# A two-layer decoder step with FFN in token halves: weight low parts and last pooling steps on VectorE, inverse root by logarithm on ScalarE, residual additions of x on GpSimd

## The reference, cut to what matters

```python
for i in range(2):
    h = rms_norm(x, norm_mix_pre[i]) * (1 + scale) + shift
    o = mla(h) if i == 0 else pool_mix(h)      # window sums of 2/4/8/16 rows, then a 256x256 product
    x = x + gate * rms_norm(o, norm_mix_post[i])
    h = rms_norm(x, norm_ffn_pre[i]) * (1 + scale_f) + shift_f
    u = h @ w_up                               # 1024 x 5632
    conv = b + u[t-2]*w0 + u[t-1]*w1 + u[t]*w2
    y = (silu(conv[:, :2816]) * conv[:, 2816:]) @ w_down
    x = x + gate_f * rms_norm(y, norm_ffn_post[i])
# pool_mix of group g with window w: (window_sum / min(pos + 1, w) - h) @ w_grp[g] * ls
```

## Time and profile before

| | |
|---|---|
| median of the runs | 2921.64 us |
| the profiled execution, its time | 2929.04 us |
| its span, first to last instruction | 2927.3 us |
| mean granted TensorE clock | 0.962 |
| TensorE matmul busy | 2586.9 us (88%) |
| VectorE busy | 1962.7 us (67%) |
| ScalarE busy | 1332.8 us (46%) |
| GpSimd busy | 518.9 us (18%) |

### The profile page before, as it was taken

The page is one execution under the profiler, slowest core; times in us unless marked ns, Lnnn a source line. Parts: engine busy times, 40 slices in busy tenths (PEclk is TensorE's granted clock), DMA queues, the critical chain, the costliest instruction groups (busy, mean ns, idle before and its releaser), DMA issues.

```text
span 2927.3 us, 49336 instructions
## 1 busy us (share of the span) xinstructions
PE 2586.9 (88%) x18538; PEld 2324.5 (79%) x18538; DVE 1962.7 (67%) x3457; ACT 1332.8 (46%) x2982; POOL 518.9 (18%) x397
## 2 busy tenths in 40 slices
PE   5979699888969888999999889999988999999995
PEld 2558466666647878999998889899887999899995
DVE  3961355655622368876668886887894887876666
ACT  5842243444412555544445545555544555444443
POOL 0000000000000354111123232313352322210112
PEclk9989899999989998999999999999999999999998
DMA  7920100000044512222232222224328222232221
GB/s 295 415 86 32 49 12 12 22 25 0 0 165 141 170 57 75 80 82 81 84 98 76 73 65 73 80 80 107 85 66 58 80 80 80 80 111 80 83 84 58
DMA packets 93281, 254.69 MB, mean 87 GB/s; under 512 B 36082, under 2 KB 40562, under 8 KB 89106
## 3 DMA queue, kind: packets, MB, share of 16 engines
q1 hardware_dynamic: 92354, 251.18, 28.1%
q10 hardware_dynamic: 720, 0.71, 0.1%
HBM read 244.79 MB, written 7.07 MB: 86 GB/s over the span
## 4 chain that ended last, share of the span: by engine, by line
PE 32%; DVE 22%; ACT 6%; issue 4%; POOL 2%; DMA 1%; ACTq 0%; DVEq 0%; POOLq 0%
PE psum L2408 5%; PE psum L2407 5%; PE psum L2406 5%; DVE t_conv L2242 5%; PE psum L2381 5%; PE psum L2383 4%; PE psum L2382 4%; DVE t_w_lo L2225 4%; DVE t_conv L2247 4%; DVE t_conv L2254 4%; ACT t_w_hi L2114 3%; DVE t_y L2274 2%; ACT t_conv L2145 1%; POOL t_stat L1820 1%; PE psum L1917 1%
## 5 line engine op out<-in xcount | busy, mean ns | idle before, releaser
L2406 PE MATMUL psum<-t_h,t_w_hi 128*128 128x272 f32 x2816 | 821.4, 292 | 2.2 <-POOL t_w_lo L2075 2.0
L2408 PE MATMUL psum<-t_h,t_w_lo 128*128 128x272 f32 x2816 | 816.8, 290 | 0.0
L2407 PE MATMUL psum<-t_h,t_w_hi 128*128 128x272 f32 x2816 | 816.3, 290 | 0.0
L2406 PEld LDWEIGHTS psum<-t_h,t_w_hi 128*128 128x128 f32 x2816 | 535.8, 190 | 4.0 <-POOL t_w_lo L2075 2.2
L2407 PEld LDWEIGHTS psum<-t_h,t_w_hi 128*128 128x128 f32 x2816 | 535.7, 190 | 1.4
L2408 PEld LDWEIGHTS psum<-t_h,t_w_lo 128*128 128x128 f32 x2816 | 535.8, 190 | 0.0
L2381 PE MATMUL psum<-t_g_hi,t_w_hi 128*128 128x272 f32 x1408 | 417.9, 297 | 127.7 <-DVE t_y L2274 112.1
L2242 DVE SCALAR_TENSOR_TENSOR t_conv<-t_u,t_taps,t_conv 128x272 f32<-128x272 f32 x704 | 357.4, 508 | 187.4 <-ACT t_conv L2145 176.6
L2075 POOL TENSOR_TENSOR t_w_lo<-t_raw,t_w_hi 128x1024 fp32r<-128x1024 f32 x96 | 240.6, 2506 | 1154.6 <-ACT t_w_hi L2114 1154.6
L2382 PE MATMUL psum<-t_g_lo,t_w_hi 128*128 128x272 f32 x1408 | 407.8, 290 | 0.0
L2383 PE MATMUL psum<-t_g_hi,t_w_lo 128*128 128x272 f32 x1408 | 407.4, 289 | 0.0
(11 more groups left out here) (204 smaller groups left out, 4166.9 us busy)
## 6 DMA issues: line engine op xcount, KB each, us to landing
t_raw<-in_ffn_w SPq DMA_DIRECT2D x264, 512.0 KB, 3.6
ada_w<-in_ada_w SPq DMA_DIRECT2D x24, 2048.0 KB, 10.9
cache<-in_cache SPq DMA_DIRECT2D x64, 320.0 KB, 5.0
t_raw<-in_wo SPq DMA_DIRECT2D x16, 512.0 KB, 3.6
pair_raw<-in_pair_w SPq DMA_DIRECT2D x8, 768.0 KB, 4.3
x<-in_x SPq DMA_DIRECT2D x1, 4352.0 KB, 22.7
x<-in_x SPq DMA_DIRECT2D x2, 2176.0 KB, 9.5
out_x_out<-x SPq DMA_DIRECT2D x4, 1088.0 KB, 6.1
```

The lines of the kernel that those rows point to most:

```text
L2406: pe.matmul(bank, t.w_hi[s][:, o], hi, start=kt == 0, stop=False)
L2407: pe.matmul(bank, t.w_hi[s][:, o], lo, start=False, stop=False)
L2408: last = pe.matmul(bank, t.w_lo[s][:, o], hi, start=False, stop=kt == KT - 1)
```

## The change

1. The low parts of all units are made by VectorE; GpSimd makes none. One semaphore `lo_ready` takes the place of two. In a pair VectorE makes the U low part right behind accumulate r=0.
2. The convolution of G is done once for both blocks (544 columns, or 480 and the 64 sample columns), behind slot 2, and SiLU is one instruction of 544 columns.
3. The reciprocal on VectorE goes; ScalarE computes exp(-0.5 * ln(mean + eps)) in two instructions instead of the square root.
4. All additions to x are GpSimd's (`every` for `even`).
5. In the pooling windows of groups 0 and 1 and of the samples, GpSimd's two last instructions are one of VectorE (`dve_finals`), two per group for the samples.
6. New ticks: `paced` puts at most one gated or modulated tile in a tick and none in a tick divisible by six; the pooling products start at tick 63 instead of 66.
7. GpSimd's loop has no order between chain ticks and pairs any more, since nothing else is in it.

```diff
+def paced(first, each=1):
+    ticks = [t for t in range(first, first + 4 * KT) if t % SLOTS]
+    whole = [t for t in ticks for _ in range(each)][:2 * KT]
+    return [whole[:KT], whole[KT:]]
...
 BETWEEN = Plan(
-    [("y", IN_ORDER, Y_SQUARES, (15, 15), (17, 18), [one_each(19), one_each(27)]),
-     ("x", IN_ORDER, [one_each(21), one_each(29)], (39, 39), (41, 42), None),
-     ("y", BY_GROUP, [two_each(68, 4), two_each(70, 4)], (84, 84), (86, 87), [one_each(88), one_each(96)]),
-     ("x", IN_ORDER, [one_each(90), one_each(98)], (108, 108), (110, 111), None)],
-    [("pool", [two_each(43), two_each(47)], 51),
-     ("ffn", [one_each(112), one_each(120)], 125)],
-    (54, 50), range(66, 82, 2))
-LAST_A = Plan([("y", IN_ORDER, Y_SQUARES, (15, 15), (17, 18), [one_each(19), one_each(27)])])
-LAST_B = Plan([("y", IN_ORDER, [[0] * KT, [1] * KT], (1, 2), (2, 3), [[3] * KT, [4] * KT])])
+    [("y", IN_ORDER, Y_SQUARES, (15, 15), paced(17), (18, 24, 30)),
+     ("x", IN_ORDER, [[t + 2 for t in paced(17)[0]], [31, 31] + list(range(32, 38))], (39, 39), None, None),
+     ("y", BY_GROUP, [two_each(65, 4), two_each(67, 4)], (81, 81), paced(83), (84, 90, 96)),
+     ("x", IN_ORDER, [[t + 2 for t in paced(83)[0]], [97, 97] + list(range(98, 104))], (105, 105), None, None)],
+    [("pool", paced(41, 2), (51, 52, 53, 54, 54)),
+     ("ffn", paced(107), (108, 114, 120, 121, 126))],
+     54, range(63, 79, 2))
+WINDOWS_BY_POOL = [[(0, 48, 51), (1, 52, 57)], [(0, 48, 50), (1, 51, 53)]]
+SAMPLE_WINDOWS = [(0, 55, 56), (1, 57, 58), (2, 59, 61), (3, 62, 64)]
+LAST_B = Plan([("y", IN_ORDER, [[0] * KT, [1] * KT], (1, 2), [[3] * KT, [4] * KT], (4, 4, 4))])
...
-            act.activation(self.stat(n, lc), t.stat_bank[lc][:, 0:T], ACT.Sqrt, scale=1.0 / D_MODEL, bias=k.eps[:])\
-               .then_inc(t.rooted, 1)
+            act.activation(self.stat(n, lc), t.stat_bank[lc][:, 0:T], ACT.Ln, scale=1.0 / D_MODEL, bias=k.eps[:])\
+               .then_inc(t.logged, 1)
...
+            act.activation(self.stat(n, lc), self.stat(n, lc), ACT.Exp, scale=-0.5).then_inc(t.inverted, 1)
-            dve.wait_ge(t.rooted, self.norm_number(n, lc) + 1)
-            dve.reciprocal(self.stat(n, lc), self.stat(n, lc)).then_inc(t.inverted, 1)
...
+    def dve_finals(self, dve, tick):
+        for g, _, at in WINDOWS_BY_POOL[self.half]:
+            if at == tick:
+                dve.wait_ge(t.window_p, self.pool_steps(g) + window_ops(self.half, g))
+                dve.scalar_tensor_tensor(h, total, 1.0 / WINDOWS[g], h, ALU.mult, ALU.subtract).then_inc(t.window_f, 1)
+        for g, _, at in SAMPLE_WINDOWS[:len(WINDOWS) * self.half]:
...
...
-        even = [kt for kt in range(KT) if kt % 2 == 0]
+        every = list(range(KT))
...
-            for n in range(N_PAIRS):
-                q, p = divmod(n, PAIRS)
-                split_lo_by_pool(pool, U, n)
-                for slot_ in range(4):
-                    chains[q + 1].pool(pool, SLOTS * p + slot_)
+            for chain in chains[1:5]:
+                for tick in range(TICKS):
+                    chain.pool(pool, tick)
...
-        def silu(act, n, lc):
-            c = t.conv[G][:, lc * T:lc * T + T]
-            act.wait_ge(t.conv_step[G], conv_end(n, lc))
-            act.activation(c, c, ACT.Silu).then_inc(t.silu_done, 1)
+        def silu(act, n):
+            act.wait_ge(t.conv_step[G], conv_end(G, n, 1))
+            act.activation(t.conv[G][:], t.conv[G][:], ACT.Silu).then_inc(t.silu_done, 1)
...
                     split_g(dve, n - 1, 1)
-                convolve(dve, G, n, 0)
                 for r in downs[0:1]:
                     accumulate(dve, r)
-                chain.dve(dve, SLOTS * p + 1)
+                split_lo(dve, U, n)
                 for r in downs[1:2]:
                     accumulate(dve, r)
-                chain.dve(dve, SLOTS * p + 2)
+                chain.dve(dve, SLOTS * p + 1)
                 for r in downs[2:3]:
                     accumulate(dve, r)
-                chain.dve(dve, SLOTS * p + 3)
+                chain.dve(dve, SLOTS * p + 2)
                 convolve(dve, G, n, 1)
...
-                chain.dve(dve, SLOTS * p + 4)
                 for r in downs[4:5]:
                     accumulate(dve, r)
-                chain.dve(dve, SLOTS * p + 5)
-                convolve(dve, U, n, 0)
+                chain.dve(dve, SLOTS * p + 3)
                 for r in downs[5:6]:
                     accumulate(dve, r)
+                chain.dve(dve, SLOTS * p + 4)
+                convolve(dve, U, n, 0)
                 multiply(dve, n, 0)
                 for r in downs[6:7]:
                     accumulate(dve, r)
                 split_g(dve, n, 0)
                 for r in downs[7:8]:
                     accumulate(dve, r)
+                chain.dve(dve, SLOTS * p + 5)
```

More of the change, by code:

```diff
@@ L1483, in __init__ @@
             of = lambda by: sum(window_ops(half, g) for g in range(len(WINDOWS)) if (g in POOL_BY_POOL) == by)
-            own |= {"window_d": of(False), "window_p": of(True) + half * sum(doublings(g) + 2 for g in range(4)),
+            own |= {"window_d": of(False), "window_p": of(True) + half * sum(doublings(g) for g in range(4)),
+                    "window_f": len(POOL_BY_POOL) + half * len(WINDOWS),
                     "product": 2 * len(WINDOWS), "pool": 1}
@@ L1555, in closed @@
         for f, (kind, _, at) in enumerate(self.plan.entries):
[L1556 removed]
+            if self.half and at[step] == tick:
                 yield f, kind
@@ L1872, in pool_sample_window @@
     def pool_sample_window(self, pool, g, step):
         t, sums = self.t, self.room.sums_s
-        tiles = slice(g * GT, (g + 1) * GT)
-        hs = self.room.hs[:, tiles]
-        n = doublings(g)
-        total = sums[(n - 1) % 2]
-        mine = self.at["window_p"] + sum(window_ops(self.half, x) for x in POOL_BY_POOL)
-        mine += sum(doublings(x) + 2 for x in range(g)) + step
-        if g == 0 and step == 0:
-            pool.wait_ge(t.put_s, self.at["entry_s"] + 1)
-        pool.wait_ge(t.window_p, mine)
@@ L1906, in pe @@
             if g in POOL_BY_POOL:
-                pe.wait_ge(t.window_p, self.at["window_p"] + sum(window_ops(self.half, x) for x in of(True)))
+                pe.wait_ge(t.window_f, self.at["window_f"] + len(of(True)))
             else:
@@ L1944, in tail_stage @@
         number = {what: o for o, what in enumerate(order)}
-        def low_by_dve(s, n):
-            return s in (G, D) or (s == "out" and n < KT)
-        by_dve = [what for what in order if low_by_dve(*what)]
-        by_pool = [what for what in order if not low_by_dve(*what)]
-        low_number = {what: i + 1 for whats in (by_dve, by_pool) for i, what in enumerate(whats)}
-        def low_ready(eng, s, n):
-            if low_by_dve(s, n):
-                eng.wait_ge(t.lo_by_dve, low_number[s, n])
-            else:
-                eng.wait_ge(t.lo_by_pool, low_number[s, n])
         def slot(s, n):
@@ L1971, in unit, with conv_steps, conv_end @@
             return io["ffn_w"][n // PAIRS // 2, n % PAIRS, s]
-        def conv_steps(n):
+        def conv_steps(s, n):
             whole, rest = divmod(n, PAIRS)
-            return sum(6 if q % 2 else 4 for q in range(whole)) * PAIRS + (6 if whole % 2 else 4) * rest
-        def conv_end(n, lc):
-            return conv_steps(n) + 2 if lc == 0 else conv_steps(n + 1)
+            each = (2, 4) if s == G else (4, 6)
+            return sum(each[q % 2] for q in range(whole)) * PAIRS + each[whole % 2] * rest
+        def conv_end(s, n, lc):
+            return conv_steps(s, n) + 2 if s == U and lc == 0 else conv_steps(s, n + 1)
         def down_tile(r):
```

192 lines of the change are left out of this document (90 added, 102 removed).

## The result

The changed kernel takes 2792.99 us (median of 4 runs, 2792.23 to 2795.12) beside 2922.53 us before (4 runs, 2919.65 to 2927.31): a ratio of 0.9556 [0.954, 0.9573], 130 us off. I had said 2805 and 118 off. The profiled execution took 2793.25 us; its span is 135.9 us shorter than that of the earlier trace rows.

The account below looks back on a forecast made before the run. TensorE's stream was taken as the bound, standing still for VectorE's late accumulations of y. Terms 29.7 + 50 + 7 + 21 + 8.5 + 1 + 1 = 118 us off gave 2804, said as 2805; range 2772 to 2850.

Parts of the forecast that it names:

- Low parts and the place of r=0: Plain pairs: without GpSimd's hold on VectorE's multiplication, TensorE's wait for accumulate r=0 goes altogether, -29.7 us.
- G convolved once: Inside a pair: both taps end at S+11.2, and two longer passes replace four, saving VectorE 0.5 us in a pair.
- the worry about r=3: Accumulate r=3, behind the long G convolution, is the next thing to be late, with a margin of 1.3 us.
- Busy pairs: Pairs beside gates, norms and modulation: three quarters of 66 us of waits go, -50 us; clock and busy time -7 us.
- Windows: Pairs with pooling window sums: VectorE's sums collide less with GpSimd, -21 us, between -5 and -30.
- Pair 1: Pair without down products: with GpSimd free of low parts it takes 14 us instead of 22.7, -8.5 us.
- the rival of the late U low part: U low part behind accumulate r=0 comes too late and stalls TensorE in every pair: slower, 2969 at L = 2; chance 0.05.
- Inverse root and additions behind the last down product: End of the kernel: 2.5 us saved without reciprocals, +2 for GpSimd's additions, block 0 starts earlier: -1 us, between -5 and +4.
- Output projection: TensorE's sum matmul waits for GpSimd: four low parts go and eight additions come, -1 us, between -5 and +4.
- All waits go: Rival: the 66 us of waits vanish whole, with larger window, clock and pair 1 gains: 153 off, 2769; chance 0.14.
- VectorE takes TensorE's place: Rival: in every pair with chain work VectorE becomes the bound, so only 58 off, 2864; chance 0.17.
- the hold stays: Rival: the multiplication's 2.5 us are its own, VectorE gains load and TensorE's wait moves: 2922; chance 0.02.

Follow-up runs that it names:

- the early entries: Changed kernel with the pooling entries two in every tick from 41 to 48, slot 0 included, instead of spread to tick 50: 2783.82 us, ratio 0.951.

## Why the prediction was right, and where its sizes were off

*What bounds the kernel, and the mechanism.* Right. The 2.51 us were a hold (0.44 once GpSimd was idle, 2.51 again with its instruction back), and the low parts alone bring 106 of the 130 us. One piece of the evidence was no evidence: the two accumulations from PSUM that took 0.78 us together started at 1375.01, when GpSimd's instruction was over (1372.50). But the trace before has 79 other accumulations that overlap one of GpSimd's, and they take 0.43 us in the median, 0.44 at most, like those that don't.

*Low parts and the place of r=0: -29.7 predicted, -35.8 measured* (12.6 and 23.2 in the two plain stretches). The waits all went. The rest is the floor: I took TensorE's busy time of a plain pair, 18.27 us, for it. It is 18.03. The 0.24 are the first matmul after the wait, 0.36 us in the earlier trace rows where one of a plain pair's 144 now takes 18.03 / 144 = 0.125: the trace counts it as busy, and a pair with a wait isn't only longer by its idle time. That was a term at nothing without a reason. I also gave this term to two causes that are alternatives, which did the sum no harm.

*G convolved once.* The times inside the pair came out (11.1 for 11.2), and the worry about r=3 was needless there; beside the chains all 8.6 us of waits for an accumulation that are left are for r=3. No gain of the edit shows in the times.

*Busy pairs: -50 for waits and -7 for the clock predicted, -54 and -21 measured.* The term that was mis-sized is the second. The sums over pairs 2 to 8, 22 to 29, 36 to 51 and 58 to 70, before and after:

```profile
sum 896.00, PE 829.21 PEld 813.53 DVE 761.49 ACT 474.12 POOL 248.90; mean PE 207.30 PEld 203.38 DVE 190.37 ACT 118.53 POOL 62.22
sum 821.30, PE 808.49 PEld 801.14 DVE 645.96 ACT 474.84 POOL 188.06; mean PE 202.12 PEld 200.28 DVE 161.49 ACT 118.71 POOL 47.01
```

Idle time fell from 66.8 to 12.8 us and busy time by 20.7, of which 1.9 are the sums' matmuls of two norms that moved into pairs 35 and 57. The forecast had -7, between 0 and -12. By the granted clock of these stretches (0.98, 0.98, 1.00 and 0.99 before, 1.00 after) some 9 us are the clock's, as an estimate; the rest is the same 0.24 us as in the plain pairs, which went with 39 of the 57 waits (39 x 0.24 = 9.4). So one wrong floor, 18.27 for 18.03, made both this term and the plain pairs' too small.

That the -50 was met is in part luck. With the low parts and the place of r=0 alone the idle time of these pairs is 23.4 us, 43 less than before; the rest went with edits that I had put at nothing inside the pairs. With the reciprocal back the idle time is 26.4 us and the pairs are 19.8 us longer, with the additions shared it is 20.6 and they are 9.5 longer. I asked whether ScalarE could carry the exponential and did not ask what 1.84 us less ahead of an accumulation is worth on VectorE, though the prediction's own rule was that the order in the queue counts, not the sum. The estimate of VectorE's fullest pair, 16.8 us, was good. Pair 26, with five gated tiles:

```profile
1545.20:1564.30 19.10, 18.39 (x146) 18.13 (x145) 17.21 (x32) 9.67 (x29) 8.29 (x9) 1.00 0.27 83
```

*Windows: -21 predicted, -12.1 measured* (71.9 to 64.8 and 73.0 to 68.0). Inside the range of -5 to -30. In fact it is more, since 32 pooling products' matmuls moved into these stretches; with the pairs behind them (33 to 35, and 57) it is 235.7 to 217.8 us, -17.9, though the 1.9 us of sums' matmuls came in as well. Those pairs alone, before and after:

```profile
sum 90.80, PE 90.80 PEld 87.33 DVE 55.49 ACT 49.41 POOL 26.96; mean PE 45.40 PEld 43.66 DVE 27.75 ACT 24.70 POOL 13.48
sum 85.00, PE 85.00 PEld 82.75 DVE 48.65 ACT 51.94 POOL 14.51; mean PE 42.50 PEld 41.38 DVE 24.33 ACT 25.97 POOL 7.25
```

GpSimd's part of the window stretches fell from 26.6 to 8.7 us as foreseen; what stayed is VectorE's load of entries and window sums in one pair, as the early entries showed by taking 7 us more out.

*Pair 1: -8.5 predicted, -2.7 measured for pairs 0 and 1* (pair 1 itself from 22.7 to 20.4). Here the rival of the late U low part is right: its first matmul waits 3.18 us for VectorE's low part where it waited for GpSimd's before, the sums' matmul 1.4 behind it, and the clock of the pair is 0.83. There are no down products in this pair to cover the time. I had counted the end of GpSimd's low parts and not the start of VectorE's.

*Inverse root and additions behind the last down product: -1 predicted, -1.5 measured* (27.1 to 25.6). The two experiments give its parts: 1.6 us for the reciprocal (I had 2.5), and 0.7 against it for the additions (I had 2). The last pair and the down products behind it lost another 2.9 us (37.5 to 34.6), which the sum did not have: one more wait for r=0 as in the plain pairs, and 1.4 that are the two forms of this stretch, which no run ties to the change. GpSimd's additions at the end, each behind its gate, and the table loads after 1000 us:

```profile
2771.03 7.23 POOL L1855 TENSOR_TENSOR x<-x,t_y 128x272 f32<-128x272 f32 x8 [2.88 <-DVE t_y L1739]
2779.96 5.32 POOL L1855 TENSOR_TENSOR x<-x,t_y 128x208 f32<-128x208 f32 x8 [1.70 <-DVE t_y L1739]
L1626 ACT ACT_TABLE_LOAD x17 | 21.8, 1283 | 0.3
L1621 ACT ACT_TABLE_LOAD x17 | 21.8, 1283 | 0.3
```

A gate and an addition in turn cost 7.23 / 8 = 0.90 us (the estimate was 0.95) and 0.67 on 208 columns (0.8). The last two rows are the table loads: 17 for the logarithm and 17 for the exponential, 1.283 us each. The Trainium skill (ScalarE: Activation LUTs, section "Table sets: the hidden batching unit") has logarithm and exponential in one set and counts one load for the two; the trace does not agree, every change from one to the other loads. Four of these loads lie behind the last down product. No run separates what the loads cost inside the pairs; with them the two instructions are still 19 us cheaper there than the reciprocal.

*Output projection: -1 predicted, -1.9 measured.*

*Sum.* Measured in the spans: output projection 1.9, pairs 0 and 1 2.7, plain pairs 35.8, busy pairs 74.7, windows with the pairs behind them 17.9, last pair 2.9, end 1.5, less 1.6 for pairs 55 and 56 (the wait in 56 grew by 2.0): 135.8 of the 135.9. The runs of before were a little faster than its profiled execution, as the prediction allowed for, and 130 remain. Pair 1 was too high by 6 and the windows by 3 to 9, the busy pairs too low by 18 and the plain ones by 6, so the 12 us of error hide larger ones. *All waits go* came nearer in the plain pairs, and 24.7 us of VectorE's waits stayed; *VectorE takes TensorE's place* holds nowhere but in the pairs with windows; *the hold stays* fell.

## What to carry to other kernels

Before a gain is added up, find the one instruction that is late and ask what stands ahead of it in its queue: removing the hold and moving the late instruction past one convolution both cured the plain pairs, and together they brought no more than one. An edit that takes a long instruction from a queue in which a critical one stands is worth something even where the engine's sum is below the bound; here 28 reciprocals of 1.84 us were 24 us, the table loads that replaced them paid for. And look at the largest single wait first even if the change does not touch it: pair 56's was 15 us for a DMA cut in pieces.
